# Hybrid decoder trunk on one core: whole experts in one transfer, with the opening and the attention stage reordered

## The chip, the cores and the metric

The kernel runs on one core of one Trainium2 chip. The metric is the device time of one execution in microseconds (us), and of the runs shown the median counts. Inputs are prepared on the host, in whatever layout the kernel asks for, and that is not part of the time.

## The reference

A trunk of two layers over x, 256 tokens by 1024, float32. Layer 0 mixes tokens by a chunked spatial gate (8 groups of 64 channels) beside a stick-breaking attention (8 heads of 64); layer 1 by a gated short convolution. Behind each mixer stands a mixture of 32 experts, of which each token uses two. RMSNorm stands ahead of each part and at the end. Cut to what matters here:

```python
# layer 0, attention, strictly causal (s < t)
z = q @ k.T / 8
A[t, s] = sigmoid(z[t, s]) * prod(1 - sigmoid(z[t, j]) for s < j < t)
b_out = A @ v
# both layers, mixture of experts (w_gate, w_up 1024 x 512, w_down 512 x 1024 per expert)
for e in range(32):
    h = silu(t @ w_gate[e]) * (t @ w_up[e])
    out += combine[:, e] * (h @ w_down[e])
```

Every expert's three matrices, 2 MiB each, are read in each layer: 64 experts, 403 MB of the 440 MB that the kernel moves.

## The kernel before, in words

Five engines run programs of their own, which meet at semaphores. SP (`block.sync`) issues nearly every load, in one order written out by hand.

**The ring.** Weights go through a ring of nine slots of 2 MiB (16 KB in each of 128 partitions). Each matrix has a number n in order of use: `L_EVEN` 0 to 6 for the blocks of layer 0's mixer, 7 on for its experts (`L_MOE[0]`), `L_ODD` for the eight blocks of layer 1's mixer, then its experts (`L_MOE[1]`). Slot n % 9 holds matrix n, and `fill` (L332) waits until the matrix nine before has been used, as `used_up` (L272) says by a semaphore and a count. Mixer blocks are split into a high and a low part for fp32r products; the high part of n goes into slot n - 2 (`LAG`), so such a slot is free later.

**The experts.** `experts(l)` (L377) loads the first three experts into the nine slots as the mixer's blocks release them; expert 27 (`EARLY`) goes into other buffers ahead of time, its gate and up by `load_early` into the parts of `scr`, `aux` and `m` that the mixer has released, its down by `load_spare`. Then a loop of turns refills the slots of three experts in each turn (`expert`, L370), matrix by matrix: gate waits for `gate_used` of the expert three before, up for `gu_ready`, down for `y_ready`. Experts 28 to 31 are loaded behind the loop, the last one's down in four quarters (L408), each with a semaphore of its own.

PE's `expert` (L1487) waits for each matrix apart, by the count of `landed` for the slot:

```python
for mat, used in enumerate((gate_used, gu_ready)):
    ...
    wait_landed(pe, n + mat, turns)
    w_of = lambda k: wide(n + mat)[:, k, :]
    gate_up(w_of, block_of, FP * mat).then_inc(used, 1)
```

Behind gate and up it scatters the expert before, turns the combine weights, gathers the next expert's tokens, waits for the hidden vector (`hhT_ready`) and for down, and runs `down` (L1453). `y_ready` rises then. Lines of the profile: L1449 are the products of gate and up, L1458 those of `down`, L1466 the scatter, L1472 the turned weights, L1478 the gather. Behind expert 28 (`DRAIN`) stands `more_experts`, for tokens over an expert's capacity, with no block to do in this input.

**The opening.** x, already transposed, and the first block come in five pieces each (`PIECES`), the second block in four (`QUARTERS`), each a slice of a larger array, so that a partition's row is contiguous (1 to 4 KB) while the next partition's row lies 8 or 16 KB further. ACT makes the high part of each piece, DVE the low part, PE multiplies (L1278).

**The attention stage** (`even` of each engine). Four heads at a time, head h in bank h % 4, with the products of keys 0 to 127 with all queries (256 columns) and of keys 128 to 255 with the later queries (128 columns) side by side. PE: `scores(0)`, the projection of the attention's values (L1323), `suffixes` of four heads (L1379 to L1381, fp32 products of a triangle of -1 and of all -1 with the softplus), the projection of the gate's v (L1323), `values(0)`, `scores(4)`, the u block (L1278), `suffixes` of the other four, the spatial gate (L1419), `values(4)` (L1392), and the output projection (L1339). DVE clips, takes softplus, masks it by `below`, and takes the minimum with `diag` behind the suffixes; ACT computes Exp, Ln and Exp. The sequence is that of the code on each engine.

Of the kernel before, what the change touches and what calls it, by code (L numbers as in the profile page):

```python
# [5 lines left out]
F32 = mybir.dt.float32  # L6
# [7 lines left out]
P = 128  # L14
# [36 lines left out]
L_MOE = [7, 7 + PER_MOE + 8]  # L51
L_ODD = 7 + PER_MOE
L_GAIN = L_MOE[1] + PER_MOE
LAST_DOWN = L_ODD - 1
APART = [L_EVEN, L_EVEN + 1, LAST_DOWN, L_ODD]
# [3 lines left out]
SPLIT = [L_EVEN + i for i in range(7)] + [L_ODD + i for i in range(8)]  # L59

# [18 lines left out]
def trunk(nc, x_in, x_turned_in, even_w_in, even_w_out, gmlp_w_s, gmlp_b_s, columns, odd_w_in,  # L79
          odd_w_out, norm_gains, router, w_gate, w_up, w_down, norm_final, out):  # L80
    with ExitStack() as ctx:
# [21 lines left out]
        att = [scr[:, 2048 + 384 * i:2048 + 384 * (i + 1)] for i in range(4)]  # L103
# [33 lines left out]
        def temp(cols):  # L137
# [29 lines left out]
        ident, below, upto, nlin, nones, diag = (sb(n, P) for n in (  # L167
            "ident", "below", "upto", "nlin", "nones", "diag"))
        below16, ones16 = sb("below16", P, BF16), sb("ones16", P, BF16)
# [21 lines left out]
        bank = [psum[:, i, :] for i in range(8)]  # L191
        GU, YB, XB, BB = bank[4], bank[5], bank[6], bank[7]


        landed = [sem(f"landed{i}") for i in range(RING)]
        gate_used, out_half = sem("gate_used"), sem("out_half")
# [35 lines left out]
        s_ready, low_ready, a_ready = sem("s_ready"), sem("low_ready"), sem("a_ready")  # L232
# [23 lines left out]
        def slot(n):  # L256
            return ring[:, (n % RING) * SLOT:(n % RING + 1) * SLOT]
# [8 lines left out]
        def lo_slot(n):  # L266
            return slot_halves[n % RING][:, :]
# [4 lines left out]
        def used_up(n):  # L272

            for l in range(2):
# [12 lines left out]
        def is_split(n):  # L287
            return L_EVEN <= n < L_MOE[0] or L_ODD <= n < L_MOE[1]

        def wait_landed(eng, n, turns=0):  # L290

            apart = sum(n > z and n % RING == z % RING for z in APART)
            eng.wait_ge(landed[n % RING], (turns + (n // RING + 1 - apart)) * 16)
# [26 lines left out]
        def rest_entry(l, e):  # L320
            return L_MOE[l] + 3 * e - 3


# [4 lines left out]
        def _(sp):  # L328
            def load(n, src, dst):
                sp.dma_start(dst, src).then_inc(landed[n % RING], 16)  # L330
# [8 lines left out]

            def load_piece(n, src, part, landed_of):  # L340
                ks = pieces(n)[part]
                ks = slice(ks.start, ks.stop)
# [1290 lines left out]
```

## Time and profile before

| | |
|---|---|
| median of 3 runs (lowest to highest) | 1086.62 us (1085.47 to 1086.83) |
| the profiled execution: its own time | 1086.43 us |
| its span in the trace | 1084.3 us |
| mean granted clock of TensorE | 0.907 |
| PE, PEld, DVE, ACT busy | 814.4, 637.4, 321.6, 192.3 us |
| moved by DMA | 439.62 MB, mean 405 GB/s |

The span is the time from the first to the last event of the trace, 2.1 us less than the execution's own time. All times in the rows are counted from the span's start. "Idle before, releaser" names what ended an engine's wait, "issue" a time in which it waited for nothing that the profile shows. Layer 0's mixer runs until about 109 us, its experts until 543, layer 1's mixer until 640, its experts until 1076.

### The profile page before, as it was taken

What the parts mean: (1) busy time and instruction counts of PE and PEld (TensorE: products, weight loads), DVE (VectorE), ACT (ScalarE), POOL (GpSimd) and SP (SyncE); (2) the same over time, 40 slices, a digit from 0 to 9 for tenths busy, and PEclk for the clock granted to TensorE, in tenths of its full rate; (3) what the DMA queues carried; (4) which work ended last, traced back from release to release, by engine and by line L of the source; (5) the groups of instructions that cost most, each with busy time, mean ns of one, the idle gap of its engine ahead of it and who ended that gap; (6) DMA issues with size and microseconds to landing.
All of it is one profiled execution on the core that took longest, in us unless ns stands there. A gap on an engine that the chain in (4) does not pass through costs nothing.

```text
span 1084.3 us, 30469 instructions
## 1 busy us (share of the span) xinstructions
PE 814.4 (75%) x13924; PEld 637.4 (59%) x13925; DVE 321.6 (30%) x801; ACT 192.3 (18%) x367; POOL 4.9 (0%) x24
## 2 busy tenths in 40 slices
PE   8999887666676766686799998966676767676864
PEld 8887665444454545464489986754454545454642
DVE  5765522111111101121177744311111111111212
ACT  5665211000000000000163331100000000000102
POOL 1000000000000000000000000000000000000000
PEclk9999999898978888888999989988978888889988
DMA  9976999999999999999998599999999999999996
GB/s 350 426 304 257 418 427 427 429 429 429 428 429 429 428 427 430 428 427 426 417 429 368 214 400 394 430 426 430 428 428 429 429 428 428 430 428 427 429 422 254
DMA packets 35872, 439.62 MB, mean 405 GB/s; under 512 B 4208, under 2 KB 4976, under 8 KB 9968
## 3 DMA queue, kind: packets, MB, share of 16 engines
q1 hardware_dynamic: 34848, 437.58, 95.9%
q10 hardware_dynamic: 976, 1.33, 0.4%
q8 instruction: 39, 0.64, 0.2%
q14 instruction: 9, 0.07, 0.0%
HBM read 437.84 MB, written 1.05 MB: 405 GB/s over the span
## 4 chain that ended last, share of the span: by engine, by line
DMA 63%; PE 30%; DVE 3%; issue 2%; ACT 1%; SPq 0%; ACTq 0%; DVEq 0%
DMA ring<-in_w_up 32%; DMA ring<-in_w_down 30%; PE psum L1278 8%; PE psum L1449 7%; PE psum L1339 4%; PE psum L1458 4%; PE psum L1323 2%; PE psum L1466 1%; PE psum L1478 1%; PE psum L1257 1%; DMA ring<-in_even_w_in 1%; PE psum L1530 1%; DVE ring_halves L782 1%; PE psum L1472 0%; PE psum L1250 0%
## 5 line engine op out<-in xcount | busy, mean ns | idle before, releaser
L1449 PE MATMUL psum<-ring,m 128*32 128x128 f32 x7936 | 310.6, 321 | 231.3 <-DMA ring<-in_w_gate 109.9
L1449 PEld LDWEIGHTS psum<-ring,m 128*32 128x32 f32 x7936 | 272.2, 130 | 277.0 <-issue 125.1
L1143 DVE TENSOR_TENSOR m<-psum,m 128x128 f32<-128x128 f32 x64 | 18.7, 292 | 575.5 <-ACT m L683 575.5
L1458 PE MATMUL psum<-ring,m 128*32 128x256 f32 x1984 | 120.8, 380 | 15.3 <-DMA ring<-in_w_down 12.1
L683 ACT ACTIVATE m<-psum 128x128 f32<-128x128 f32 x64 | 17.7, 277 | 530.1 <-PE psum L1449 530.1
L1278 PE MATMUL psum<-scr_halves,ring_halves 128*128 128x256 f32 x768 | 107.0, 286 | 4.4 <-DVE ring_halves L782 3.8
L1278 PEld LDWEIGHTS psum<-scr_halves,ring_halves 128*128 128x128 f32 x768 | 100.9, 194 | 5.0 <-DVE ring_halves L782 4.2
L1458 PEld LDWEIGHTS psum<-ring,m 128*32 128x32 f32 x1984 | 66.2, 110 | 62.1 <-issue 21.9
L1466 PE MATMUL psum<-m 32*128 32x256 f32 x1056 | 80.7, 422 | 2.1 <-DVE m L1148 1.1
L782 DVE TENSOR_TENSOR ring_halves<-ring,ring_halves 128x2048 fp32r<-128x2048 f32 (+2 forms) x37 | 68.6, 1885 | 11.6 <-ACT ring_halves L530 11.3
L1478 PE MATMUL psum<-x,m 128*32 128x256 f32 x1024 | 69.8, 385 | 2.2 <-issue 1.5
L530 ACT ACTIVATE ring_halves<-ring 128x2048 fp32r<-128x2048 f32 (+2 forms) x37 | 57.3, 1581 | 38.7 <-PE psum L1278 28.8
L1466 PEld LDWEIGHTS psum<-m 32*128 32x128 f32 x1056 | 51.3, 199 | 21.3 <-issue 14.8
L1117 DVE STREAM_TRANSPOSE m<-psum 128x256 f32<-128x256 f32 x64 | 28.8, 450 | 91.3 <-PE psum L1478 91.3
L689 ACT ACTIVATE m<-psum 128x256 f32<-128x256 f32 x62 | 23.8, 383 | 169.0 <-PE psum L1458 169.0
L1478 PEld LDWEIGHTS psum<-x,m 128*32 128x32 f32 x1024 | 27.1, 109 | 25.6 <-issue 13.3
L1126 DVE TENSOR_SCALAR m<-count,pos,cw 128x128 f32<-128x128 f32 x128 | 38.3, 342 | 1.2 <-issue 1.2
L685 ACT ACTIVATE m<-psum 128x256 f32<-128x256 f32 x64 | 24.5, 383 | 73.8 <-PE psum L1472 73.7
L1339 PE MATMUL psum<-ring_halves,aux_halves 128*128 128x512 f32 x96 | 32.7, 395 | 0.0
L1112 DVE TENSOR_SCALAR m<-count,pos,rstd 128x32 f32<-128x32 f32 x128 | 32.2, 296 | 0.8 <-DVE extra L1100 0.7
L1472 PE MATMUL psum<-ident,m 128*128 128x128 f32 x128 | 28.0, 300 | 0.0
L1120 DVE TENSOR_TENSOR m<-m,gains 128x256 f32<-128x256 f32 x64 | 27.2, 425 | 2.2
(188 smaller groups left out, 498.4 us busy)
## 6 DMA issues: line engine op xcount, KB each, us to landing
ring<-in_w_gate SPq DMA_DIRECT2D x62, 2048.0 KB, 40.5
ring<-in_w_up SPq DMA_DIRECT2D x62, 2048.0 KB, 40.7
ring<-in_w_down SPq DMA_DIRECT2D x60, 2048.0 KB, 41.1
ring<-in_odd_w_in SPq DMA_DIRECT2D x5, 2048.0 KB, 26.2
ring<-in_even_w_in SPq DMA_DIRECT2D x3, 2048.0 KB, 20.5
ring<-in_even_w_out SPq DMA_DIRECT2D x2, 2048.0 KB, 30.8
spare<-in_w_down SPq DMA_DIRECT2D x2, 2048.0 KB, 23.2
ring<-in_w_down SPq DMA_DIRECT2D x8, 512.0 KB, 37.6
```

The costliest lines, as they stand in the source:

```text
L530: act.activation(hi_slot(n)[:, c], slot(n)[:, c], ACT.Copy).then_inc(w_hi, 1)
L782: dve.tensor_tensor(lo_slot(n)[:, c], slot(n)[:, c], hi_slot(n)[:, c].bitcast(F32), ALU.subtract).then_inc(w_lo, 1)
L1112: last = dve.tensor_scalar(sel[:, t, CAP * i:CAP * (i + 1)], ranks, pos[:, bass.ds(at(e, t), 1)], rstd[:, t:t + 1], ALU.is_equal, ALU.mult)
L1117: return dve.transpose(xg[:, i, :, :], XB[:, 0:DP].rearrange("p (q k) -> p k q", k=K))
L1126: last = dve.tensor_scalar(wsel[:, t, :].rearrange("p (n c) -> p n c", n=NP), count[:, 1:CAP + 1].unsqueeze(1).to_broadcast([P, NP, CAP]), ...
L1278: return pe.matmul(bank[banks[c // 2]][:, (c % 2) * S:(c % 2 + 1) * S], w[a][:, k, P * c:P * (c + 1)], h[b][:, k, :], start=k == 0 and a + ...
L1339: last = pe.matmul(bank[2 * t + c][:, :], mix[a][:, 4 * r + j, P * t:P * (t + 1)], w[b][:, j, 512 * c:512 * (c + 1)], start=r == 0 and j = ...
L1449: last = pe.matmul(GU[CAP * part:CAP * (part + 1), lo:lo + FP], block_of(k), w_of(k)[:, FP * part:FP * (part + 1)], start=k == 0, stop=k = ...
L1458: last = pe.matmul(YB[CAP * part:CAP * (part + 1), 0:DP], hhT[:, CAP * f:CAP * (f + 1)], w[:, f, DP * part:DP * (part + 1)], start=f == 0, ...
L1466: last = pe.matmul(bank[part][:, DP * t:DP * (t + 1)], cmb[r, P * t:P * (t + 1)], yy[r, :], start=False, stop=False, skip_group_check=True)
L1472: last = pe.transpose(BB[:, P * t:P * (t + 1)], wsel[:, t, :], ident[:, :])
L1478: last = pe.matmul(XB[CAP * part:CAP * (part + 1), 0:DP], sel[:, t, CAP * i:CAP * (i + 1)], x[:, t, DP * part:DP * (part + 1)], start=t == ...
```

## The change

**Experts.** The three matrices of an expert lie behind one another in each partition's row on the host (`expert_weights`, 48 KB per partition and expert). From the second turn on, so from expert 3, an expert is loaded by one transfer into three neighbouring slots (`whole`), which waits for `y_ready` of the expert that was there, and PE waits once, ahead of gate, for a semaphore of the whole third of the ring. This holds for experts 3 to 30 but for expert 27, 27 in each layer. The first three experts, expert 27 and the last one are loaded matrix by matrix as before. PE's first turn stands unrolled ahead of its loop. Slots are numbered anew (`place(n) = (n + 2) % 9`), so that an expert's three slots are neighbours, and one number, `HOLE`, stays without a matrix behind the odd mixer's; with it the order of the first loads of layer 1 changes.

**Opening.** The pieces of x, of the first and second block and of the first odd block, and the quarters of the last down, are each stored as one contiguous run.

**Attention.** Two heads of the same half (even or odd) share a bank: banks 0 and 1 hold the products of 256 columns of two heads each, banks 2 and 3 those of 128. The causal mask is added by PE, as an identity times `diag` in bf16, so that DVE no longer masks. The softplus of the later keys is split into a high and a low part in fp32r for their suffixes. Scores and suffixes stand between the two halves of a projection.

The diff, cut to its core (`...` marks what is left out):

```diff
-L_MOE = [7, 7 + PER_MOE + 8]
+L_MOE = [7, 7 + PER_MOE + 9]
+HOLE = L_ODD + 8
+FINE = TRI
+def place(n):
+    return (n + 2) % RING
+def is_whole(e):
+    return FINE <= e < NE - 1 and e != EARLY
...
 def used_up(n):
+    if n == HOLE:
+        return used_up(L_ODD + 1)
...
-            def expert(l, b, i):
-                e = b * TRI + i
-                for mat, used in enumerate((gate_used, gu_ready, y_ready)):
-                    n = L_MOE[l] + 3 * i + mat
-                    sp.wait_ge(used, after(l, e - TRI))
-                    load(n, matrix(l, e, mat), buffer(n, mat))
+            def whole(l, e, i, former):
+                sp.wait_ge(y_ready, after(l, former))
+                at = place(L_MOE[l] + 3 * i) * SLOT
+                sp.dma_start(ring[:, at:at + 3 * SLOT], expert_weights_in[l, e]).then_inc(whole_landed[third(l, i)], 16)
 
             def experts(l):
+                if l:
+                    first(l, 2, 2)
+                    load_spare(l)
                 first(l, 0, 0)
+                first(l, 0, 1)
                 if l == 0:
-                    first(l, 0, 1)
-                load_spare(l)
-                if l == 1:
-                    first(l, 0, 1)
+                    load_spare(l)
                 first(l, 0, 2)
                 first(l, 1, 0)
-                first(l, 1, 1)
+                if l == 0:
+                    first(l, 1, 1)
                 sp.wait_ge(*((even_lo, 6), (pb_ready, 4))[l])
                 load_early(l, 0, 0, 1)
-                first(l, 1, 2)
-                first(l, 2, 1)
+                first(l, 1, 2 - l)
+                first(l, 2, 1 - l)
                 load_early(l, 1, 0, 2)
-                first(l, 2, 0)
-                first(l, 2, 2)
+                first(l, 1 + (l == 0), 2 * l)
+                first(l, 2, 2 - l)
                 load_early(l, 1, 1, 2)
                 with sp.Fori(1, TURNS) as b:
                     for i in range(TRI):
-                        expert(l, b, i)
+                        whole(l, b * TRI + i, i, b * TRI + (i - TRI))
+                for e in range(DRAIN, NE - 1):
+                    whole(l, e, (e - 1) % TRI, e - 4)
...
+                for j in range(NP):
+                    sp.dma_start(tall(n + 2)[:, j, :], last_down[l, j]).then_inc(quarter_landed[j], 16)
...
+                act.activation(nlin_r[:, :], nlin[:, :], ACT.Copy)
+                act.activation(nones_r[:, :], nones[:, :], ACT.Copy)
...
+                logs(1)
+                hi(5)
...
+                gelu_u(0)
+                weights(1)
+                gelu_u(1)
...
+                def softplus(g):
+                    for n, i in enumerate((LATE, 0, 1)):
+                        dve.wait_ge(ln_ready, 3 * g + n + 1)
+                        dve.tensor_tensor(piece(i), score[i], piece(i), ALU.max).then_inc(sp_ready, 1)
+                    dve.wait_ge(low_hi_made, g + 1)
+                    dve.tensor_tensor(low_lo, att[LATE], low_hi.bitcast(F32), ALU.subtract).then_inc(low_lo_made, 1)
...
+                    for keys in range(2):
+                        for r in range(2):
+                            n = S - P * keys
+                            diagonals = bank[2 * keys + r][:, 0:2 * n].rearrange("p (b t) -> p b t", b=2)[:, :, 0:P]
+                            last = pe.matmul(diagonals, ident16[:, :], diag16[:, :].unsqueeze(1).to_broadcast([P, 2, P]),
+                                             start=False, stop=False, skip_group_check=True)
+                    last.then_inc(z_ready, 1)
+                def suffixes(g):
+                    for r in range(2):
+                        pe.wait_ge(sp_ready, 3 * g + r + 2)
+                        pe.matmul(bank[r][:, :], nlin[:, :], att[r], start=False, stop=False, skip_group_check=True)
+                    pe.wait_ge(low_lo_made, g + 1)
+                    for r in range(2):
+                        for half in (low_hi, low_lo):
+                            two = half[:, S * r:S * (r + 1)]
+                            later = bank[r][:, :].rearrange("p (b t) -> p b t", b=2)[:, :, P:S]
+                            last = pe.matmul(later, nones_r[:, :], two.rearrange("p (b t) -> p b t", b=2), start=False,
+                                             stop=half is low_lo, skip_group_check=True)
+                        last.then_inc(s_ready, 1)
+                    for half in (low_hi, low_lo):
+                        for r in range(2):
+                            last = pe.matmul(bank[2 + r][:, 0:S], nlin_r[:, :], half[:, S * r:S * (r + 1)], start=False,
+                                             stop=half is low_lo, skip_group_check=True)
+                    last.then_inc(s_ready, 1)
...
+                tokens(L + 2, (4, 5), vv_ready, first_scores)
+                tokens(L + 3, (6, 7), v_ready, lambda: suffixes(0))
                 values(0, 6)
                 scores(4)
-                channels(L + 4, (4, 5), u_ready)
+                channels(L + 4, (4, 5), u_ready, between=lambda: suffixes(1))
...
+                def wait_weights(mat):
+                    if not rest and not isinstance(T, int):
+                        if mat == 0:
+                            pe.wait_ge(whole_landed[third(l, i)], (T + (whole_count(l, TRI + i) - 1)) * 16)
+                    elif rest and is_whole(e):
+                        if mat == 0:
+                            pe.wait_ge(whole_landed[place(n) // 3], whole_count(l, e) * 16)
+                    else:
+                        wait_landed(pe, n + mat)
...
-                with pe.Fori(0, TURNS) as T:
+                for i in range(TRI):
+                    expert(l, 0, i)
+                with pe.Fori(1, TURNS) as T:
                     for i in range(TRI):
                         expert(l, T, i)
...
+        "x_turned": in_pieces(given["x"][0].T.reshape(P, K, S), PIECES),
+        "even_first": in_pieces(even_in[2], PIECES),
+        "even_second": in_pieces(even_in[3], QUARTERS),
+        "odd_first": in_pieces(odd_in[2], QUARTERS),
+        "expert_weights": np.concatenate([given[name].reshape(2, NE, P, SLOT) for name in ("w_gate", "w_up", "w_down")], axis=3),
+        "last_down": given["w_down"][:, NE - 1].reshape(2, P, NP, D).transpose(0, 2, 1, 3),
```

## Rows read from the trace of the kernel before

**Rows 1.** The page: the chain by engine, and GB/s in 40 equal slices.

```profile
GB/s 350 426 304 257 418 427 427 429 429 429 428 429 429 428 427 430 428 427 426 417 429 368 214 400 394 430 426 430 428 428 429 429 428 428 430 428 427 429 422 254
...
DMA 63%; PE 30%; DVE 3%; issue 2%; ACT 1%; SPq 0%; ACTq 0%; DVEq 0%
```

**Rows 2.** The chain of waits in the experts: start us, us, what.

```profile
836.25 1.97 PE psum L1458 x32
...
1012.47 1.93 PE psum L1458 x32
```

**Rows 3.** SP's timeline: start us, us, line, operation (first refills of both layers).

```profile
122.70 0.35 SPq L330 DMA_DIRECT2D ring<-in_w_gate  x1
...
131.05 0.33 SPq L330 DMA_DIRECT2D ring<-in_w_down  x1
...
152.61 0.33 SPq L330 DMA_DIRECT2D ring<-in_w_down  x1
...
160.28 0.33 SPq L330 DMA_DIRECT2D ring<-in_w_down  x1
...
655.81 0.34 SPq L330 DMA_DIRECT2D ring<-in_w_gate  x1
...
662.70 0.33 SPq L330 DMA_DIRECT2D ring<-in_w_down  x1
```

**Rows 4.** Stretches: busy us of each engine, granted clock, DMA share, GB/s.

```profile
120.00:130.00 10.00, 7.76 (x185) 5.69 (x187) 6.96 (x29) 0.99 (x4) 0.00 (x0) 1.00 1.02 418
656.00:658.00 2.00, 2.00 (x60) 1.58 (x52) 1.67 (x10) 0.28 (x1) 0.00 (x0) 1.00 0.68 162
```

**Rows 5.** The chain of waits, the up matrix of expert 8 in layer 0.

```profile
171.44 40.13 DMA ring<-in_w_up
```

**Rows 6.** PE's timeline, experts 26 to 31 of layer 0, expert 31 of layer 1.

```profile
480.88 1.93 PE L1458 MATMUL psum<-ring,m 128*32 128x256 f32 x32 [0.58 <-DMA ring<-in_w_down]
...
508.51 3.67 PE L1449 MATMUL psum<-ring,m 128*32 128x128 f32 x72 [6.08 <-issue]
...
518.50 0.82 PE L1449 MATMUL psum<-ring,m 128*32 128x128 f32 x21
...
531.32 1.95 PE L1449 MATMUL psum<-ring,m 128*32 128x128 f32 x64 [1.82 <-DMA ring<-in_w_gate]
...
536.18 1.95 PE L1449 MATMUL psum<-ring,m 128*32 128x128 f32 x64 [1.46 <-DMA ring<-in_w_up]
...
541.34 0.64 PE L1458 MATMUL psum<-ring,m 128*32 128x256 f32 x8 [0.48 <-DMA ring<-in_w_down]
...
1062.90 1.96 PE L1449 MATMUL psum<-ring,m 128*32 128x128 f32 x64 [2.95 <-DMA ring<-in_w_gate]
```

**Rows 7.** A stretch behind an idle PE, columns as in rows 4.

```profile
508.50:512.50 4.00, 3.67 (x72) 3.40 (x72) 0.00 (x0) 0.00 (x0) 0.00 (x0) 0.61 1.03 430
```

**Rows 8.** The chain of waits in the attention stage.

```profile
23.55 11.52 PE psum L1278 x96
...
48.62 0.43 PE psum L1379 x2
...
52.14 10.91 PE psum L1323 x48
...
87.25 22.04 PE psum L1339 x96
```

**Rows 9.** PE's timeline: waits in the attention stage, and cold code in expert 0.

```profile
35.93 1.58 PE L1370 MATMUL psum<-m 64*128 64x256 f32 x16 [0.88 <-DVE m L858]
...
78.52 0.67 PE L1379 MATMUL psum<-scr,nlin 128*128 128x256 f32 x2 [0.83 <-DVE scr L872]
...
83.61 1.97 PE L1419 MATMUL psum<-m 128*64 128x128 f32 x32 [1.25 <-DVE m L916]
...
126.40 0.42 PE L1449 MATMUL psum<-ring,m 128*32 128x128 f32 x5 [2.19 <-issue]
```

**Rows 10.** The opening as a stretch, columns as in rows 4.

```profile
0.80:12.70 11.90, 7.92 (x42) 7.50 (x42) 4.48 (x7) 6.08 (x11) 3.42 (x18) 1.00 0.85 284
```

More of the change, by code:

```diff
@@ L59, with rest_entry, entry, third @@
 SPLIT = [L_EVEN + i for i in range(7)] + [L_ODD + i for i in range(8)]
+def rest_entry(l, e):
+    return L_MOE[l] + 3 * e - 3
+def entry(l, e):
+    return L_MOE[l] + 3 * e if e < EARLY else rest_entry(l, e)
+def place(n):
+    return (n + 2) % RING
+def third(l, i):
+    return place(L_MOE[l] + 3 * i) // 3
+def is_whole(e):
+    return FINE <= e < NE - 1 and e != EARLY
+SINGLE = [z for z in SPLIT if z not in (L_EVEN, L_EVEN + 1, L_ODD)]
+for layer in range(2):
+    for expert in range(FINE):
+        SINGLE += [entry(layer, expert) + mat for mat in range(3) if expert < TRI or mat]
+    SINGLE += [entry(layer, NE - 1) + mat for mat in range(2)]
+SINGLE.append(L_GAIN)
+WHOLE = [(layer, expert) for layer in range(2) for expert in range(TRI, NE) if expert < FINE or is_whole(expert)]
+def single_count(n):
+    return sum(z <= n and place(z) == place(n) for z in SINGLE)
+def whole_count(l, e):
+    return sum((zl, ze) <= (l, e) and place(entry(zl, ze)) == place(entry(l, e)) for zl, ze in WHOLE)
 def pieces(n):
@@ L256, in slot @@
         def slot(n):
-            return ring[:, (n % RING) * SLOT:(n % RING + 1) * SLOT]
+            return ring[:, place(n) * SLOT:(place(n) + 1) * SLOT]
         def wide(n):
@@ L287, in is_split, with wait_landed @@
         def is_split(n):
[L288 to L293, printed above, removed]
+            return n in SPLIT
+        def wait_landed(eng, n):
+            eng.wait_ge(landed[place(n)], 16 * single_count(n))
         @contextmanager
@@ L329, in load @@
             def load(n, src, dst):
-                sp.dma_start(dst, src).then_inc(landed[n % RING], 16)
+                sp.dma_start(dst, src).then_inc(landed[place(n)], 16)
             def fill(n, src, dst):
@@ L338, in fill, with piece_of @@
                 load(n, src, dst)
+            def piece_of(flat, ks, width):
+                run = flat[P * width * ks.start:P * width * ks.stop]
+                return run.rearrange("(p k f) -> p k f", p=P, f=width)
             def load_piece(n, src, part, landed_of):
                 ks = pieces(n)[part]
-                ks = slice(ks.start, ks.stop)
-                sp.dma_start(wide(n)[:, ks, :], src[:, ks, :]).then_inc(landed_of[part], 16)
+                sp.dma_start(wide(n)[:, ks.start:ks.stop, :], piece_of(src, ks, 512)).then_inc(landed_of[part], 16)
             def load_early(l, i, part, parts):
-                w = (w_gate, w_up)[i][l, EARLY].rearrange("(p k) f -> p k f", k=K)
+                w = matrix(l, EARLY, i)
                 n = HK // parts
@@ L1293, in channels @@
                         last_product(c, K - 1, last)
+                        if between and c == 2:
+                            between()
                     return
@@ L1325, in tokens @@
                     last.then_inc(ready, 1)
+                    if t == 0:
+                        between()
             def project_out(n, l, wait_rows):
```

202 lines of the change are left out of this document (88 added, 114 removed).

## The prediction

> **What bounds the kernel now.** I read the page's chain first: 63% of it is DMA and 30% PE, and the GB/s line stands near 428 except in three places: the first slice, slices 3 and 4, and slices 22 and 23 [rows 1]. So the kernel is a stream of weights that runs full, and it is longer than that stream by the time in which DMA has no buffer to fill. A change pays if it makes the full stream faster or its holes shorter, and it costs what it adds to the holes or puts behind the last byte.
>
> The chain in the experts gives the pace: `down` of every third expert starts on a landing, at 836.25 and four periods later at 1012.47 [rows 2]. That is 44.055 us for nine matrices, 4.895 us each, 14.685 us per expert, 428.4 GB/s. PE needs about 7.7 us per expert where it does not wait: SP gets the down slots of experts 2 and 3 back at 152.61 and 160.28 [rows 3].
>
> The holes come from the ring. SP's timeline shows the first refill of each layer waiting for expert 0: its gate slot is refilled at 122.70 and 655.81, its down slot at 131.05 and 662.70 [rows 3]. At those points all twelve expert buffers have been given out, and DMA has next to nothing left: at 656 to 658 it moves 162 GB/s, while layer 0 just gets through without a hole, 418 GB/s in 120 to 130 [rows 4]. That 162 also says how long an issue takes until bytes flow: 1.2 of the 2 us are missing after an issue at 655.81, so I use 1.5 to 2 us.
>
> **The change part by part.** I call y(e) the moment at which expert e's `down` is done and `y_ready` rises.
>
> 1. *First refill, layer 0.* Before, the refill for expert 3 starts with its gate at 122.70, after `gate_used`. After, the whole of expert 3 waits for y(0), 131.05, which is 8.35 us later [rows 3]. What covers it is the backlog of first loads. From one side: no hole in rows 4, so the backlog lasted until 124.6 at least, and all 8.35 could be a hole. From the other: the up matrix of expert 8 is the 17th refill and lands at 171.44 + 40.13 = 211.57 [rows 5]; 17 transfers of 4.895 and 1.9 us of latency before it put the end of the backlog at 126.5. So the new hole is 6.5 to 8.35 us: I take **+7.4**, the middle. Behind the waiting SP stand only the next wholes; PE, which next needs expert 3, has experts 1 and 2 to do meanwhile.
>
> 2. *First refill, layer 1.* 662.70 less 655.81: **+6.9**. DMA was already empty there [rows 4], so nothing covers it. In layer 1 the order of the first loads changes as well (expert 2's down goes first, into the slot that the new numbering leaves free), but each waits for one of the same releases of the odd mixer, with the same bytes behind each; I cost that at nothing. The cover is that the first loads reach the last release with a hole before it anyway (slice 23); were it gone, one matrix late would cost at most its 4.9 us.
>
> After the first whole there is no further hole: y(2) comes 21.6 us after y(0) [rows 3], before the two wholes then given out (14.7 us each) are through. In steady state two other experts, 29 us of stream, cover a PE time of 10 us.
>
> 3. *Rate.* 27 experts per layer, 54 in all, go as one transfer in place of three. What a transfer costs beside its bytes: the last expert's down comes in four quarters, each with as many rows as a whole matrix; its up landed at 536.18 and the last quarter at 541.34 [rows 6], 5.16 us against 4.895 for one transfer of the same bytes. Three more transfers cost 0.27 us, 0.09 each, and two fewer save 0.18. I take 0.15, since part of the 0.27 may be the quarters' short strided rows: 54 x 0.15 = **-8.0**. Bounds: nothing gained (48 KB rows appear nowhere in this trace), and -12, if the saving is half as large again. The Trainium skill, "DMA: Bandwidth & Descriptors", section "Where 436 GB/s comes from", gives a ceiling of 435.2 GB/s; by that a 6 MB transfer saves 0.23 us at most, 12 us in all, and no run here shows it.
>
> 4. *Behind the last landing.* Now PE starts an expert's gate only when its down is there too. In steady state this is free, as PE waits anyway. It is not free in experts 26 to 31, for expert 27 is read from other buffers without a wait, and PE must do both in one expert's stream time. In layer 0 PE starts expert 26's `down` at 480.88, on a landing, with 1.93 us left to do [rows 6]. After the change that landing starts the whole expert: 7.7 us at full clock and about 1.8 more, since after 6 us of idle the granted clock was 0.61 for 4 us, a mean of the two levels 1.2 and 2.4 GHz [rows 7]. So y(26) moves from 482.8 to 490.4, and the rest follows without a gap: experts 27, 28 and the walk to expert 29's first product take 508.51 less 482.8 = 25.7 us [rows 6], which gives 516.1; expert 29 takes 10 (518.50 less 508.51) and ends at 526.1. Expert 30 has just landed then (before, the next gate landed at 531.32 [rows 6], one matrix of 4.9 later: 526.4). Its work was 10.9 us long (from 518.50, two stalls in it), so 537.3; expert 31 takes 1.95 for gate, 1.5 for scatter and turn, 1.95 for up, 1.2 for the hidden vector and 1.95 for `down`, 8.6 in all: 545.9 against 542.0. Without the stalls, while PE waits at the head of expert 30, it is 543.9. I take **+3.0**. In layer 1 PE waited 2.95 us for expert 31's gate, 1.82 in layer 0 [rows 6], so it has over 1 us more of slack: **+1.5**. Bounds for both together 0.5 and 9.
>
> 5. *Attention.* PE executes the suffixes in 3.52 us per four heads (48.62 to 52.14 [rows 8]). The new ones are, per four heads, two fp32 products of 512 columns (1.74 us, by 0.43 for one of 256 columns, which the trace records as two), eight of 256 columns in fp32r at the 0.12 of the projections (11.52 us for 96 [rows 8]), and four masks on the diagonal in bf16, which no row shows at this size, at 0.12 as well: 3.2. That is 0.7 us less in all. The waits of PE before 35.93, 78.52 and 83.61 (0.88, 0.83, 1.25 us [rows 9]) are what the new places of scores and suffixes, between two halves of a projection, can remove. That would make -3.7, if neither ACT nor DVE became late. But ACT gets one more table load (1.28 us) between gelus and exponentials, and when I follow the new order by hand, the output projection starts some 1.3 us before today's 87.25 [rows 8]. I take **-1.5**, bounds -3.7 and +1.
>
> 6. *Opening.* The pieces of x and of the first, second and odd first blocks are stored so that each is one contiguous run; the rows written stay 1 to 4 KB. Until PE's steady start at 12.72 DMA moves 284 GB/s, at a busy share of 0.85 [rows 10]; in the next slices it moves 426 [rows 1]. If the contiguous source helps, the third piece lands earlier; what waits for it is a fixed chain of 3 us on ACT and DVE. Nothing to -3, I take **-1.0**, a third of what the full rate would give.
>
> 7. *With one answer.* T = 0 unrolled ahead of the loop is code for three experts more per layer. Cold code shows idle time without a releaser (2.19 before 126.40 [rows 9]); experts 0 to 2 have it before too, and experts 3 to 5, now cold as well, have 14.7 us of stream for 8 + 3: nothing. SP's fewer issues: nothing, it mostly waits. A code fetch that meets a row of 48 KB instead of 16 KB stays inside the same slack.
>
> Sum: 7.4 + 6.9 - 8.0 + 3.0 + 1.5 - 1.5 - 1.0 = **+8.3 us** on the profiled execution's own 1086.43, so 1094.7. The median of the runs lies 0.2 above that: 1094.8 within rounding.
>
> **The rivals.**
> A. *No gain of rate*: DMA's overhead goes by the byte and not by the transfer, or the hardware cuts 48 KB rows so that the wholes do no more than the three did. For it: long stretches all show the same rate. Against: the four quarters. 1094.8 + 8.0 = 1102.8.
> B. *The tail is free and the rate better*: PE's stalls vanish when it waits at an expert's head, and the transfers save 0.2 us. 1094.8 - 4.5 - 2.7 = 1087.6; with a good opening 1085.
> C. *The other side: the first refills are covered.* The first loads would still be in flight at y(0) in both layers, because they move later in the new order. Then 14.3 us fall away: 1080.5. It decides where the last first load ends after 131.05 and 662.70, over 6 us later than worked out. Against it: the 162 GB/s [rows 4]. For it: layer 0 has no hole at 120 to 130.
>
> **How the numbers follow.** A measurement of this kernel tells changes of about 0.2%, 2.2 us. Chances: forecast 0.52 (1089 to 1100), A 0.18 (1099 to 1107), B 0.20 (1083 to 1090), C 0.10 (1078 to 1084). Slower by over 0.2% (above 1088.8) takes the forecast, A and a third of B: 0.77. Within 0.2%: nearly half of B, 0.10. Faster: C and the rest of B, 0.13. The range 1086 to 1104 leaves out C, part of B and the upper end of A.
>
> **What would show it.** Right: no DMA between 657 and about 664 and a like hole in layer 0; a period of 43.6 us for three experts; expert 31's last products bound by PE and not by a landing. Wrong: a period still 44.05 (A); no hole at expert 0 (C); the output projection starting after 87.25 would void the term of attention. A hole behind the second refill would break the premise that only the first is late.

## The result and the profile after

The change makes the kernel slower: **1101.4 us** median of 4 runs (1098.29 to 1104.58) against 1086.05 of 4 runs of the kernel before (1085.00 to 1086.83), a ratio of 1.0146 (1.0132 to 1.0159). That is +15.3 us, inside the range given (to 1104), on the side given, and 7 us above the forecast of +8.3. It lies outside the narrower band of the forecast itself (1089 to 1100) and inside that of rival A (1099 to 1107), so the band does not tell the two apart; the traces have to. The profiled execution of after is its slowest run, 1104.58, so the traces differ by 18.2 us. The runs of after lie 6 us apart, those of before within 2; in the three blocks below the kernel before itself scatters by 3 to 7 us.

The page of after, GB/s in 40 slices, packets, queue 1 and the chain by engine, stands beside [rows 1]:

```profile
GB/s 361 428 277 315 291 430 426 431 437 433 433 431 428 433 440 430 433 431 425 414 423 284 221 398 340 430 427 433 439 433 431 430 430 439 433 435 430 427 419 118
...
q1 hardware_dynamic: 19296, 437.57, 93.3%
...
DMA 51%; PE 41%; issue 4%; ACT 2%; DVE 2%; SPq 0%; ACTq 0%; DVEq 0%
```

Three things are to be seen. The long stretches stand a little higher than 428. Slice 5 falls from 418 to 291 and slice 25 from 394 to 340: the two holes. And the last slice has 118 where it had 254: the transfers end further ahead of the kernel's end than they did. The chain says the same, 51% DMA and 41% PE where it was 63% and 30%, with 4% "issue": more of the end hangs on PE, and part of that on PE waiting for nothing that the trace shows.

**The first refills.** SP's timeline of after, both layers (start us, us, line, operation), against [rows 3]:

```profile
130.27 8.00 SPq L416 DMA_DIRECT2D ring<-in_expert_weights  x2
...
668.89 0.35 SPq L416 DMA_DIRECT2D ring<-in_expert_weights  x1
```

and stretches of after (PE, PEld, DVE, ACT, POOL busy us, granted clock, DMA share, GB/s), against [rows 4]:

```profile
122.00:124.00 2.00, 1.40 (x26) 0.77 (x16) 1.69 (x10) 0.28 (x1) 0.00 (x0) 1.00 0.28 109
124.00:126.00 2.00, 1.39 (x11) 0.70 (x14) 1.11 (x4) 0.28 (x1) 0.00 (x0) 0.89 0.03 8
126.00:130.00 4.00, 4.00 (x56) 1.98 (x52) 1.81 (x6) 0.10 (x1) 0.00 (x0) 0.63 0.00 0
...
132.00:134.00 2.00, 2.00 (x68) 1.79 (x60) 0.00 (x1) 0.28 (x1) 0.00 (x0) 1.00 0.55 221
...
664.00:666.00 2.00, 0.87 (x14) 0.33 (x10) 1.50 (x8) 0.38 (x1) 0.00 (x0) 1.00 0.15 53
666.00:668.00 2.00, 2.00 (x40) 1.20 (x40) 1.39 (x5) 0.00 (x0) 0.00 (x0) 1.00 0.00 0
668.00:670.00 2.00, 2.00 (x72) 1.77 (x64) 0.86 (x4) 0.38 (x1) 0.00 (x0) 1.00 0.72 205
...
120.00:130.00 10.00, 8.79 (x162) 5.46 (x155) 6.41 (x27) 0.66 (x2) 0.00 (x0) 0.83 0.26 104
200.00:480.00 280.00, 185.29 (x3736) 143.99 (x3734) 49.41 (x158) 20.64 (x59) 0.00 (x0) 0.85 1.00 433
```

The last of these stretches in before:

```profile
200.00:480.00 280.00, 189.58 (x3720) 139.16 (x3720) 48.28 (x154) 20.49 (x59) 0.00 (x0) 0.86 1.01 428
```

In layer 0 nothing is moved from 126 to 130, and from 120 to 130 it is 104 GB/s against 418. The bytes missing from 122 to 132 (109, 8, 0, 0 and 369 GB/s in steps of 2 us, against a full 430) are worth some 7.7 us, and the 221 GB/s from 132 to 134 are another 1.0. In layer 1 those missing from 664 to 672 (53, 0, 205 and 197) are worth about 6 us; but before has a dip of its own there, 344 and 162 GB/s from 654 to 658, worth some 1.7. The rate in the middle of layer 0 is 433 GB/s against 428.

**Behind the last landings.** PE's timeline of after, experts 25 and 26, the spare expert 27 and the first products of expert 29 in layer 0, against [rows 6]:

```profile
469.29 5.37 PE L1519 MATMUL psum<-ring,m 128*32 128x128 f32 x128 [4.13 <-DMA ring<-in_expert_weights]
...
483.82 5.37 PE L1519 MATMUL psum<-ring,m 128*32 128x128 f32 x128 [4.99 <-DMA ring<-in_expert_weights]
...
499.11 1.91 PE L1528 MATMUL psum<-spare,m 128*32 128x256 f32 x32
...
516.54 1.08 PE L1519 MATMUL psum<-ring,m 128*32 128x128 f32 x16 [3.36 <-issue]
522.05 4.64 PE L1519 MATMUL psum<-ring,m 128*32 128x128 f32 x112 [4.43 <-issue]
```

PE idles for 4.99 us and then does gate and up in 5.37 us; the same 128 products take 3.49 at full clock (a row of the chain below); the granted clock is 0.68 from 483.8 to 489.2 and 1.00 from 1032.4 to 1035.9. Expert 27's `down` starts 15.3 us behind the landing of expert 26. Before, it was 7.7 (488.57 behind 480.88). From there on PE waits for no transfer at all in either layer, and yet it idles. The chain of after, experts 26 to 31 of layer 1 (start us, us, what):

```profile
1022.87 5.37 PE psum L1519 x128
...
1032.41 3.49 PE psum L1519 x128
...
1044.08 3.08 issue
...
1055.41 7.38 issue
1062.79 4.44 PE psum L1519 x75
...
1090.29 1.98 PE psum L1528 x32
```

The last weights land while this chain runs. Of after, the same columns as above:

```profile
1078.00:1082.00 4.00, 2.87 (x43) 1.66 (x44) 0.70 (x2) 0.66 (x2) 0.00 (x0) 1.00 0.63 247
1082.00:1086.00 4.00, 4.00 (x106) 3.37 (x100) 1.39 (x4) 0.38 (x1) 0.00 (x0) 1.00 0.07 28
```

The full stream ends near 1080 (242 GB/s from 1079 to 1080, 172 in the next us), and PE ends the last `down` at 1092.3, some 12 us behind it. Before, the stream falls off near 1070 (274 GB/s from 1070 to 1071) and the last `down` ends at 1074.0.

**Bookkeeping.** Marks of the two profiled executions, in us:

| mark | before | after | difference |
|---|---|---|---|
| output projection starts | 87.25 | 84.53 | -2.7 |
| layer 0: expert 26 has landed | 480.88 | 483.82 | +2.9 |
| layer 0: last `down` ends (its quarter from 541.34, its 32 products from 548.58) | 542.0 | 550.5 | +8.5 |
| layer 1: expert 26 has landed | 1012.47 | 1022.87 | +10.4 |
| layer 1: last `down` starts | 1072.05 | 1090.29 | +18.2 |

So the tails, from the landing of expert 26 to the last `down`, cost 5.6 us in layer 0 (8.5 less 2.9) and 7.8 in layer 1 (18.2 less 10.4), together 13.4 of the 18.2.

### The profile page after: what moved, and what is told of

Read it like the earlier page. It is cut to its first block, busy times and chain, and to the rows that moved or that the text cites. A ratio compares the mean times of both kernels' runs of the same rounds, so it can differ in the third digit from the quotient of the medians.

```text
span 1102.8 us, 30134 instructions
## 1 busy us (share of the span) xinstructions
PE 819.2 (74%) x13908; PEld 654.8 (59%) x13909; DVE 316.0 (29%) x783; ACT 193.5 (18%) x358; POOL 6.0 (1%) x26
## 4 chain that ended last, share of the span: by engine, by line
DMA 51%; PE 41%; issue 4%; ACT 2%; DVE 2%; SPq 0%; ACTq 0%; DVEq 0%
DMA ring<-in_expert_weights 50%; PE psum L1519 12%; PE psum L1327 8%; PE psum L1528 5%; PE psum L1392 4%; PE psum L1536 3%; PE psum L1548 3%; PE psum L1374 2%; PE psum L1542 1%; PE psum L1306 1%; DMA ring<-in_even_first 1%; PE psum L1612 0%; ACT ring_halves L570 0%; PE psum L1299 0%; PE psum L1424 0%
## 5 line engine op out<-in xcount | busy, mean ns | idle before, releaser
L1519 PE MATMUL psum<-ring,m 128*32 128x128 f32 x7936 | 316.5, 332 | 250.4 <-DMA ring<-in_expert_weights 217.9
L1519 PEld LDWEIGHTS psum<-ring,m 128*32 128x32 f32 x7936 | 294.7, 136 | 281.5 <-issue 202.4
L1528 PEld LDWEIGHTS psum<-ring,m 128*32 128x32 f32 x1984 | 65.3, 111 | 51.5 <-issue 7.0
L1548 PE MATMUL psum<-x,m 128*32 128x256 f32 x1024 | 72.3, 397 | 2.5 <-issue 1.3
L834 DVE TENSOR_TENSOR ring_halves<-ring,ring_halves 128x2048 fp32r<-128x2048 f32 (+2 forms) x37 | 68.7, 1886 | 13.2 <-ACT ring_halves L570 13.1
## 6 DMA issues: line engine op xcount, KB each, us to landing
ring<-in_odd_w_in SPq DMA_DIRECT2D x5, 2048.0 KB, 26.8
```

Source lines behind the costliest of these rows:

```text
L834: dve.tensor_tensor(lo_slot(n)[:, c], slot(n)[:, c], hi_slot(n)[:, c].bitcast(F32), ALU.subtract).then_inc(w_lo, 1)
L1519: last = pe.matmul(GU[CAP * part:CAP * (part + 1), lo:lo + FP], block_of(k), w_of(k)[:, FP * part:FP * (part + 1)], start=k == 0, stop=k = ...
L1528: last = pe.matmul(YB[CAP * part:CAP * (part + 1), 0:DP], hhT[:, CAP * f:CAP * (f + 1)], w[:, f, DP * part:DP * (part + 1)], start=f == 0, ...
L1548: last = pe.matmul(XB[CAP * part:CAP * (part + 1), 0:DP], sel[:, t, CAP * i:CAP * (i + 1)], x[:, t, DP * part:DP * (part + 1)], start=t == ...
```

## The experiments

**Theory.** The whole transfers do three things, each with a price of its own: they are issued late (a hole at each layer's first refill, 14 us), they are waited for late (PE begins expert 26 only when all of it is there, 9 to 11 us of tail), and they are faster (8 us back). Opening and attention give 2 to 3 us. **Rivals:** the time lies in what came along, the new order of the first loads, the slots and the unrolled code; or the tail is slow because of PE's stalls in cold code, above all at the walk (`more_experts`), and not because of the late start.

All but two kernels are the changed one with a set `WHOLES` of the experts that go as one transfer. The others go matrix by matrix through the same slots, with PE waiting for each matrix, and turns in which the two kinds meet are unrolled (the second turn where experts 3 to 5 are fine, that of experts 24 to 26 where one of these is), so these kernels also run more code for the first time in a layer:

```diff
-    return FINE <= e < NE - 1 and e != EARLY
+    return e in WHOLES and e != EARLY
...
-            def whole(l, e, i, former):
+            def whole(l, e, i, former, like=None):
+                if not is_whole(e if like is None else like):
+                    for mat, used in enumerate((gate_used, gu_ready, y_ready)):
+                        n = L_MOE[l] + 3 * i + mat
+                        sp.wait_ge(used, after(l, former))
+                        load(n, matrix(l, e, mat), buffer(n, mat))
+                    return
```

Each block of runs has its own runs of the kernel before. A difference in us is the ratio times that kernel's median. The ratio is not always the quotient of the two medians: `fine_first` is +10.9 by its ratio and +9.1 by the medians, `fine_tail` +8.5 and +6.6, `fine_both` -4.2 and -5.4, the others agree within 1 us. The result above, +15.3, is by the medians; its ratio gives 15.9. Each ratio has an interval of some 2 us to either side (3 in `fine_26` and `fine_rest`), and a difference between two kernels more.

### First and last experts: four kernels on one chip (kernel before 1087.12)

`all_matrices`: nothing is whole, all else of the change stays.

```diff
+WHOLES = []
```

> The changed kernel with every expert in three transfers and three waits again, opening and attention new. Theory (two holes at the first refills, a tail, a gain of rate, 2.5 us of opening and attention): the kernel before less 2.5, near 1083.5 us, period of three experts back at 44.05 us. Rival (opening and attention are worth nothing, or the unrolled turn costs what they give): 1086 or above.

Measured: 1085.19 us, ratio 0.9983 (0.9965 to 1.0002), -1.9 us. What the change carries besides its transfers costs nothing. It seems to bring about 2 us, though the interval just reaches 1. The first rival falls.

`fine_first`: the first refills (experts 3 to 5) go matrix by matrix.

```diff
+WHOLES = list(range(6, 31))
```

> Only experts 3 to 5 go back to matrix by matrix, each load behind the use of its own slot; experts 6 to 30 stay whole. Theory (the late first refill costs 7.4 and 6.9 us): 1101.4 less 14.3 plus 0.9 for the six lost gains of rate, 1088. No hole in DMA at expert 0. Rival (the time went mainly into the tail, and the hole is filled again by a later slack): 1096 or above.

Measured: 1096.23 us, ratio 1.0100 (1.0081 to 1.0119), +10.9 us. The profiled run, 1093.49, is the lowest of its four. This buys only 4 to 6 us over the changed kernel, by ratios or medians, less than the 14 of the two holes: the rival's figure (1096 or above), and not the theory's 1088.

`fine_tail`: whole up to expert 23, matrix by matrix behind it.

```diff
+WHOLES = list(range(3, 24))
```

> Only experts 24 to 26 and 28 to 30 go back to matrix by matrix; 3 to 23 stay whole and the first refills stay late. Theory (PE falls behind because expert 26 starts only when it is whole; the last byte lands 9 to 11 us before PE's end): about 11 us less and 1.8 of rate lost, 1092. Rival (PE's tail is made of code fetches that are slow whatever the weights do): 1099 to 1103.

Measured: 1093.72 us, ratio 1.0078 (1.0059 to 1.0096), +8.5 us: 7 less than the changed kernel's +15.3, near the 1092 expected.

`fine_both`: both edits.

```diff
+WHOLES = list(range(6, 24))
```

> Experts 3 to 5, 24 to 26 and 28 to 30 matrix by matrix, 6 to 23 whole. If the two costs are separate they add up: 1101.4 - 13.4 - 9.4 = 1078.6, below both kernels. If the holes and the tail are one slack seen twice: no better than the better of the two alone, 1088.

Measured: **1081.71 us** of 7 runs (1080.93 to 1083.25), ratio 0.9961 (0.9949 to 0.9974), -4.2 us: faster than both kernels, though 3 us above the 1078.6 expected. Of the 4.2, 1.9 are those of `all_matrices`; the whole transfers in the middle are worth the other 2.3 (3.5 by medians), and the two intervals overlap. Its page and its stretches:

```profile
GB/s 353 427 287 313 408 427 437 433 433 430 433 433 435 430 435 422 424 427 425 418 428 351 217 398 421 435 428 433 432 437 433 431 431 431 431 425 425 427 424 230
```

```profile
120.00:130.00 10.00, 8.78 (x158) 5.60 (x154) 6.24 (x27) 0.66 (x2) 0.00 (x0) 0.83 1.03 425
655.00:675.00 20.00, 17.78 (x427) 13.01 (x423) 7.15 (x23) 2.09 (x6) 0.00 (x0) 1.00 1.01 425
```

The fifth slice is back at 408 and the 25th at 421; 120 to 130 has 425 GB/s where after has 104, and the first refills of layer 1 run at 425 too. Slices 7 to 15 keep their 430 to 437. Between `fine_tail` and `fine_both` only the first refills differ, and that is 12.7 us. Between `fine_first` and `fine_both` only the tail does, and that is 15.1. Singly, the two edits bring 4 to 6 and 7 us to the changed kernel, and together 19.5: most of the gain of each comes only when the other is there too. They do not add up as expected.

### Issue and start apart (kernel before 1085.62)

These have no whole transfer, so that each half of the lateness stands alone. `after_again` is the changed kernel once more, written with the set `WHOLES = list(range(3, 31))`.

> The changed kernel once more, instruction for instruction, on the chip and in the rounds of the next three: 15 us above the kernel before. It also gives a second profile, to see how much of the tail is chance: the first profiled execution was its slowest of four.

Measured: 1102.43 us, ratio 1.0148 (1.0131 to 1.0165), +16.1 us: the result again.

`late_issue`: three transfers, but all behind `y_ready`.

```diff
-                    for mat, used in enumerate((gate_used, gu_ready, y_ready)):
+                    for mat, used in enumerate((y_ready, y_ready, y_ready)):
```

> All experts in three transfers, but all three behind y_ready of the expert before in the slots; PE waits matrix by matrix. Only SP's wait is the changed kernel's. Theory (SP's wait costs the two holes and nothing else): the version with three fine waits, 2 us under the kernel before, plus 14, so 12 above the kernel before. Rival (a late issue also thins the stream in steady state or at the end): over 16 above.

Measured: 1096.46 us, ratio 1.0097 (1.0080 to 1.0114), +10.5 us, so 12.4 above `all_matrices`; expected were 12 above the kernel before, and the rival's 16 did not come. Its trace has a hole too, 82, 0, 8 and 131 GB/s from 662 to 670 in steps of 2 us. The mere lateness of the issue makes the holes, at either size of the transfer.

`late_start`: issued as before the change, but PE waits for all three matrices ahead of gate, in experts 3 to 30.

```diff
+                    late = True and TRI <= like < NE - 1
+                    for m in ((range(3) if mat == 0 else ()) if late else (mat,)):
+                        pe.wait_ge(landed[place(at + m)], count(single_count(at + m)))
```

> All experts in three transfers, each issued as its own slot comes free; PE waits for all three ahead of gate. Only PE's wait is the changed kernel's. Theory (PE's wait costs the tail of both layers, 9 to 11 us, and no hole): 7 to 9 above the kernel before. Rival (the tail needs the late issue or the long rows too): within 2 us of it.

Measured: 1090.21 us, ratio 1.0047 (1.0030 to 1.0064), +5.1 us, so 7.0 above `all_matrices`, both tails together. That is below the 7 to 9 expected above the kernel before, and well above the rival's 2. It is also only half of the 15.1 that the whole transfers cost in the tail by `fine_first` against `fine_both`: late start alone does not account for that figure, and no run splits the rest.

`three_late`: both.

> Both waits of the changed kernel, but three transfers per expert: what is left against the changed kernel is the transfer alone. Theory (0.15 us per expert, 54 of them): 8 above the changed kernel, 23 above the kernel before, with a period of 44.05 us. Rival (long rows give nothing, or cost in the tail by slower code fetches): 0 to 4 above the changed kernel.

Measured: 1106.05 us, ratio 1.0191 (1.0174 to 1.0208), +20.7 us, 22.6 above `all_matrices`, a little more than the 19.4 of the two alone. It is the changed kernel in all but its transfers, so the difference, 4.6 us (3.6 by medians), is what the whole transfers give back, some 2.5 us either way. Expected were 8, and 0 to 4 by the rival; it lies between. In the profiled runs the whole transfers bring 3.5 and 3.1 us from the first refill's issue to the landing of expert 26 (353.6 and 354.0 us in after, 357.0 and 357.1 in `three_late`), and lose 3.4 and 2.4 from there to the last `down`. PE's timeline of `three_late`, experts 24 to 26 of layer 0:

```profile
456.73 6.35 PE L1532 MATMUL psum<-ring,m 128*32 128x128 f32 x128 [5.33 <-DMA ring<-in_expert_weights]
471.41 5.37 PE L1532 MATMUL psum<-ring,m 128*32 128x128 f32 x128 [4.16 <-DMA ring<-in_expert_weights]
486.09 5.34 PE L1532 MATMUL psum<-ring,m 128*32 128x128 f32 x128 [5.14 <-DMA ring<-in_expert_weights]
```

14.68 us per expert, as before the change; in after it is 14.53 (483.82 less 469.29). Both show PE coming out of 4 to 5 us of idle and taking 5.4 us for what takes 3.49 at full clock.

### Where in the tail (kernel before 1086.07)

`fine_26`: expert 26 alone goes matrix by matrix, with the turn of experts 24 to 26 unrolled.

```diff
+WHOLES = list(range(3, 26)) + [28, 29, 30]
```

> The changed kernel with expert 26 alone matrix by matrix (its turn unrolled behind the loop). Theory (PE's lag is made at expert 26, whose work now starts 7.6 us late ahead of expert 27, which needs no landing): most of the tail goes, and what is left is expert 30's, 2 to 4 us per layer: about 8 us above the kernel before. Rival (the lag is made where experts 28 to 30 wait as wholes): 13 or more above it.

Measured: 1105.87 us, ratio 1.0175 (1.0145 to 1.0205), +19.0 us: no faster than the changed kernel, and a miss, since 8 was expected and the rival's 13 or more came. Expert 27's `down` does come earlier (494.21 against 499.11), but expert 28, a whole one, then makes PE wait again, 2.1 us at 499.26, and the stall ahead of expert 29 is 8.3 us long, where after has 3.4. Taking the late start away at expert 26 is not enough: the whole expert behind the spare one brings a wait anew.

`fine_rest`: all of them behind 26 go matrix by matrix, 26 stays whole.

```diff
+WHOLES = list(range(3, 27))
```

> The counterpart: experts 28 to 30 matrix by matrix, expert 26 whole. Theory: the lag of expert 26 stays, and by then PE is behind the landings, so their waits cost little: 13 to 15 us above the kernel before. Rival: 8 or less.

Measured: 1095.55 us, ratio 1.0089 (1.0060 to 1.0118), +9.7 us, 6 below the changed kernel. Expected were 13 to 15, by the rival 8 or less. With expert 27's `down` just as late as in after (15.3 us behind the landing in layer 0), PE comes from that `down` to the last one in 48.0 and 47.1 us in place of 49.5 and 52.1. That is 6.5 us less, and the stalls of the table below are 6.5 less as well (20.3 against 26.8). That points to the size of the transfers behind expert 26, although PE waits for none of them; single tails scatter by 2 us and more.

`no_walk`: the changed kernel without the code for tokens over an expert's capacity; the input has none. It leaves out the calls of `more_experts` on PE, DVE and ACT and SP's loop for them.

```diff
-                         more_experts(l)
```

> The changed kernel without the walk over experts with more tokens than their capacity (more_experts, on PE, DVE, ACT and SP; with this input it finds no block). It leaves out that part of the computation. Theory (behind expert 26 PE and not the stream sets the end, so 7.5 us less on PE per layer show in the time until a landing binds again): 9 to 11 us less than the changed kernel, 5 to 7 above the kernel before. Rival (the end hangs on landings there too): less than 3 us less.

Measured: 1092.52 us, ratio 1.0062 (1.0043 to 1.0082), +6.7 us, 9.4 below `after_again` by the two ratios and 8.6 below the result of the change. Expected were 9 to 11 less. What PE waited for in the tail of layer 0 (us in total, times, longest), first in after from 469 to 560, then in `no_walk` from 500 to 560:

```profile
PE psum L1519 <- issue: 10.4, 4, 4.4
PE psum L1519 <- DMA ring<-in_expert_weights: 9.1, 2, 5.0
PE psum L1528 <- issue: 1.9, 1, 1.9
```

```profile
PE psum L1503 <- DMA ring<-in_expert_weights: 8.8, 2, 6.0
...
PE psum L1512 <- issue: 0.5, 1, 0.5
```

The 9.1 us of after all lie ahead of expert 27's `down`. Behind it after has 12.3 us without a releaser and none on a landing; `no_walk` has 0.5 and 8.8. Without the walk PE is quick enough to wait for the stream again, which is why only 9 of the 27 us of stalls come back.

`before_no_walk`: the same cut from the kernel before.

> The same left out of the kernel before. Theory (its end hangs on the last landings, PE has slack): within 1 us of the kernel before. Rival (the walk costs its time in every kernel): 8 us or more below it.

Measured: 1084.83 us, ratio 0.9984 (0.9972 to 0.9997), -1.7 us. Its stalls fall from 12.1 and 10.2 us per layer to 1.7 and 2.6, and the time hardly moves, if by a little more than the 1 us expected. Before the change most of the stalls were under the stream, and after it they help to set the end.

**Stalls in the tail.** Idle time of PE without a releaser, from expert 27's first product to the last `down`, layers 0 and 1, in us, added up from PE's timelines:

| kernel | expert 26 | transfers behind it | stalls |
|---|---|---|---|
| before | 16 KB rows | 16 KB | 12.1, 10.2 |
| all_matrices | 16 KB | 16 KB | 8.7, 11.0 |
| late_issue | 16 KB | 16 KB | 8.6, 11.9 |
| late_start | 16 KB | 16 KB | 10.3, 11.4 |
| three_late | 16 KB | 16 KB | 5.1, 12.6 |
| fine_both | 16 KB | 16 KB | 11.1, 12.2 |
| fine_tail | 16 KB | 16 KB | 13.8, 11.7 |
| fine_rest | 48 KB | 16 KB | 10.6, 9.7 |
| fine_first | 48 KB | 48 KB | 12.6, 12.2 |
| after | 48 KB | 48 KB | 12.5, 14.3 |
| after_again | 48 KB | 48 KB | 14.6, 13.2 |
| fine_26 | 16 KB | 48 KB | 15.5, 16.1 |

The four with 48 KB rows in flight in the tail have a mean of 13.9 us per layer, the eight others 10.7. The values scatter by as much as that difference, so 3 us is a size and not a measurement, and that the rows make the stalls longer is likely and not shown.

## Why the prediction was right, and where its size was off

The forecast had the signs of its large terms right: two holes, a gain of rate, a cost behind the last landing. Its size came out at +8.3 against +15.3. By ratios, the runs that isolate a term give 12.4 for the late issue (forecast 14.3), 7.0 for the late start (4.5), 3.2 more when both are together (nothing), 4.6 back from the whole transfers (8.0) and 1.9 back from all else (2.5): 16.1 in all, with an error of some 2 us on each. So the tail was costed too low and the gain too high, and the late issue a little too high, which offset part of it by luck.

1. *First refill of layer 0*, forecast 7.4: measured 7.7 to 8.7 in missing bytes. The refill was issued at 130.27, 0.8 us earlier than the 131.05 of before, while the backlog ended some 3 us earlier than worked out (404 GB/s from 120 to 122, 109 from 122 to 124). Of the 2.7 us by which the output projection starts earlier, only 0.8 are left at expert 0's `down`: PE stalls for 1.21 us ahead of 124.61, and its gather and `down` take 1.94 and 2.73 us at a granted clock of 0.63, where before they took 1.07 and 1.91. So the hole ate a part of what opening and attention gave. That is why expert 26 landed 2.9 us later and not 1.3 (7.4 less 2.5 less 24 x 0.15).
2. *First refill of layer 1*, forecast 6.9: about 6 in missing bytes, of which before has some 1.7 already. `late_issue` gives 12.4 for both layers, and `fine_tail` against `fine_both` 12.7, against a forecast of 14.3. Rival C, that they are covered, is refuted. The hole is not where I put it: I said 657 to 664, and it lies at 664 to 671, because layer 0 ends 8.5 us later; expert 0's `down` in layer 1 is then 6.2 later (668.89 against 662.70).
3. *Rate*, forecast 0.15 us per expert: 14.53 against 14.685 in the trace, exactly that. Rival A is refuted, though the median lies in its band. But the 8 us count only where a landing sets the pace. The six transfers behind expert 26 bring nothing, since PE lags there; that is 0.9 of the 8. Up to expert 26 the traces show 6.6 against `three_late`. By the ratios 4.6 are left, and in the profiled runs the tail of after is the longer one by 5.8 (that run of after is its slowest): part of what the transfers gain is lost again behind it. The ceiling that the Trainium skill gives ("DMA: Bandwidth & Descriptors", section "Where 436 GB/s comes from"), 435.2 GB/s, stands just above the 433 GB/s measured over 280 us; single slices of the page of after read up to 440, so these rows do not show it as a hard limit.
4. *Behind the last landing*, forecast 3.0 and 1.5: **this term was mis-sized**. It was 5.6 and 7.8 in the profiled run, 8.9 more in all, and 7.0 by `late_start`, which leaves the long rows out. The mechanism was right to the tenth up to expert 27: 7.6 us of lag at expert 27's `down` (15.3 against 7.7), with 5.37 us for the products of expert 26 at the low clock. What failed is the rest of the step. I took the walk from expert 27 to expert 31 over from before with its stalls, let two of them vanish against expert 30's wait, and read layer 1's wait of 2.95 us for expert 31's gate as slack. In before that time was made of landings, and the stalls lay partly under them: taking them away gave 1.7 us (`before_no_walk`). Once PE lags 7.6 us nothing is under a landing any more, and the same cut gives 9.4 (`no_walk`), until landings bind again. The stalls are also longer by some 3 us per layer in the kernels with 48 KB rows in flight, within their scatter. I had named this in step 7, "a code fetch that meets a row of 48 KB", and had put it inside a slack that the tail does not have. Layer 1 had no more slack than layer 0: its stalls alone are 14.3 us.
5. *Attention and opening*, forecast -2.5 together: the projection starts 2.7 us earlier in the profiled run, and 0.8 to 4.5 earlier in the twelve profiles of the new attention (86.43 down to 82.73 against 87.25). `all_matrices` as a whole is 1.9 faster. Part of a gain on the first stage is a hole earlier in layer 0, as in point 1. The opening moves 309 GB/s from 0.8 to 12.7 us, where it had 284 [rows 10].
6. *With one answer.* The refills behind the first are covered, as forecast: the middle of layer 0 runs at 433 GB/s over 280 us.

Rival B, a free tail, is refuted, and the forecast's own mechanism holds, with its step 4 beyond the upper bound that I gave (9 us for both layers) in the profiled run. The time stayed inside the range because the range was wide enough for that. What stays open: `fine_first` alone is 4 to 6 us better than the changed kernel, while the same edit on top of a fine tail is worth 12.7. Its tail is PE-bound as after's is. A hole filled there should still come through in full, since the tail follows the landing of expert 26, and the profiled runs differ by 11.1 us (1093.49 against 1104.58); but these are the lowest run of one kernel and the highest of the other. The medians say less, and the runs with a PE-bound tail scatter by 2 to 6 us, which does not cover all of it. Open as well is why a whole tail costs 15.1 us by `fine_first` against `fine_both` where a late start costs 7.0. Nor is it shown that the longer stalls are code fetches: the trace gives them no releaser, and only their place (code run for the first time in the layer) and `no_walk` speak for it. `no_walk` takes out the walk's own branches and register work together with its code, and the profile counts neither as busy, so it can't tell these apart.

## What to carry to other kernels

Before transfers are made coarser, look at two places and not at the mean rate: where the queue runs dry when the last buffer is released, and what work must follow the last landing. A coarse transfer is issued by its last part's release and used by its last part's landing, and in a full stream both are free, so use fine transfers for the first refills and the last experts and coarse ones between: here that is 4.2 us faster than the kernel before and 20 faster than the change. Nearly half of the 4.2 comes with the opening and attention, so the coarse middle is a small gain, and the fine ends are what avoids the loss. Idle time without a releaser that costs nothing today is a debt: a small lag in front of it makes a part of it due, here 9 us.

## What the runs showed of the hardware

A 6 MB transfer in rows of 48 KB saves 0.15 us against three in rows of 16 KB (14.53 against 14.68 us per expert, 433 against 428 GB/s), in a queue that never empties. After 4 to 5 us of idle PE takes 5.37 us, at a granted clock of 0.68, for 128 products that take 3.49 at 1.00: a wait put in front of a block makes the block itself longer. After the stall of 7.38 us the clock stays at the lower level of 1.2 GHz for the whole block, 0.50 from 1062.8 to 1067.2, and 75 products take 4.44 us. From 126 to 130 in after, with the DMA quiet, the granted clock is 0.63, a mean of 1.2 and 2.4 GHz, behind an idle PE as in [rows 7]. And in code that runs for the first time in a layer, beside a full stream, PE stands still for up to 8.3 us at a time without a releaser, 5 to 16 us in a layer's tail; 0.5 is left of it in layer 0 of `no_walk`. What these stalls are is not shown.
